# Gate maps of a PEER block: five of eight scaled one-hot rows on VectorE, none on GpSimd, all evictions on ScalarE

## The reference

```python
def peer(h, w_pq, sub_keys, expert_u, expert_v):
    q = (h @ w_pq).reshape(B, S, PEER_HEADS, 2, PEER_QHALF)          # 8 heads
    s = jnp.einsum('bshjd,hjnd->bshjn', q, sub_keys)
    v1, i1 = lax.top_k(s[..., 0, :], 16)
    v2, i2 = lax.top_k(s[..., 1, :], 16)
    ...                                                             # 16 best sums v1 + v2
    idx = ...                                                       # i1 * 128 + i2 of the chosen
    gate = jax.nn.softmax(top_s, axis=-1)
    ...
    a = jnp.einsum('tkd,td->tk', expert_u[idx], h)
    w = gate * jax.nn.gelu(a)
    return jnp.einsum('tk,tkd->td', w, expert_v[idx])
```

## Time and profile before

| | us |
|---|---|
| median of 3 runs | 2202.58 (2202.4 to 2205.08) |
| the profiled execution, its own time | 2205.34 |
| its span, first to last instruction | 2203.6 |
| gates stage, first one-hot work to last eviction | 729.66 to 897.94, that is 168.28 |
| engines busy over the span | PE 91%, DVE 60%, ACT 31%, POOL 23% |

### The profile page before, as it was taken

One profiled execution on the slowest core, in us unless ns is written; L12 is line 12 of the kernel. 1 busy time (PEld: TensorE's weight loads), 2 busy tenths in 40 slices (PEclk: granted clock), 3 DMA queues, 4 the chain that ended last, 5 costly groups with the idle time before them and its releaser, 6 DMA issues.

```text
span 2203.6 us, 25778 instructions
## 1 busy us (share of the span) xinstructions
PE 2012.5 (91%) x9280; PEld 1654.8 (75%) x9280; DVE 1316.8 (60%) x2260; ACT 679.1 (31%) x1074; POOL 499.6 (23%) x305
## 2 busy tenths in 40 slices
PE   5998876969987777899999999999999999999997
PEld 4777555747775777788788888888888888888886
DVE  6545677349997899655445544554555455445544
ACT  4113342342322788412222212222221222122212
POOL 1877424027776677100000000000000000000000
PEclk7899678979998999999999999999999999999999
DMA  8243000422232666754322422342233224322430
GB/s 320 105 191 153 1 0 3 150 95 71 78 115 86 210 206 196 251 187 151 131 95 95 172 113 95 114 171 95 95 137 149 95 95 152 133 95 95 168 118 38
DMA packets 124158, 276.65 MB, mean 126 GB/s; under 512 B 4816, under 2 KB 70352, under 8 KB 116560
## 3 DMA queue, kind: packets, MB, share of 16 engines
q1 hardware_dynamic: 124112, 276.10, 34.5%
HBM read 233.10 MB, written 42.99 MB: 125 GB/s over the span
## 4 chain that ended last, share of the span: by engine, by line
PE 58%; DVE 0%; ACT 0%; DVEq 0%; issue 0%; ACTq 0%
PE bank L1815 27%; PE bank L1841 26%; PE bank L1830 6%; DVE u_raw L1802 0%; DVE rows L1788 0%; ACT L1727 0%; DVE u L1736 0%; DVEq L1588 0%; ACT u L1680 0%; ACT v_raw L1723 0%; DVE rows L1768 0%; DVE rows L1779 0%; ACT act_out L1705 0%; ACTq L1588 0%; DVE rstd L1798 0%
## 5 line engine op out<-in xcount | busy, mean ns | idle before, releaser
L1815 PE MATMUL bank<-actT,u 128*128 128x512 f32 x2592 | 593.7, 390 | 6.9 <-DVE u L1736 4.2
L1841 PE MATMUL bank<-v_parts,w 128*128 128x512 f32 x2496 | 570.0, 389 | 0.0
L1815 PEld LDWEIGHTS bank<-actT,u 128*128 128x128 f32 x2592 | 487.6, 188 | 108.7 <-DVE u L1736 4.3
L1841 PEld LDWEIGHTS bank<-v_parts,w 128*128 128x128 f32 x2496 | 468.6, 188 | 97.1
L1768 DVE TENSOR_TENSOR rows<-rows,bank 128x512 f32<-128x512 f32 x208 | 142.4, 687 | 256.8 <-PE bank L1841 256.8
L1687 ACT ACTIVATE v_parts<-v_raw 128x1024 fp32r<-128x1024 f32 x104 | 109.7, 1055 | 450.9 <-DVE rows L1768 450.4
L1388 PE MATMUL bank<-actT,hl 128*128 128x512 f32 x864 | 212.8, 406 | 31.0 <-POOL hl L1238 27.7
L1747 DVE TENSOR_TENSOR weighed<-act_out,group_gates 128x512 f32<-128x512 f32 x105 | 72.7, 692 | 270.9 <-ACT act_out L1691 270.9
L1388 PEld LDWEIGHTS bank<-actT,hl 128*128 128x128 f32 x864 | 167.6, 197 | 70.1 <-POOL hl L1238 18.2
L1744 DVE TENSOR_TENSOR v_parts<-v_raw,v_parts 128x1024 fp32r<-128x1024 f32 x128 | 156.3, 1221 | 91.9 <-DMA group_gates<-expert_gates 32.3
L1691 ACT ACTIVATE act_out<-bank 128x512 f32<-128x512 f32 x104 | 62.2, 598 | 401.9 <-PE bank L1815 401.9
(11 more groups left out here) (239 smaller groups left out, 2039.3 us busy)
## 6 DMA issues: line engine op xcount, KB each, us to landing
u_raw<-in_u SPq DMA_DIRECT2D x27, 2048.0 KB, 7.4
v_raw<-in_v SPq DMA_DIRECT2D x26, 2048.0 KB, 7.4
expert_gates<-gates SPq DMA_DIRECT2D x16, 2048.0 KB, 8.7
group_gates<-expert_gates SPq DMA_DIRECT2D x32, 1024.0 KB, 6.8
wada<-in_w_ada SPq DMA_DIRECT2D x24, 1024.0 KB, 6.7
v_raw<-in_v SPq DMA_DIRECT2D x24, 512.0 KB, 3.5
raw<-in_u SPq DMA_DIRECT2D x20, 512.0 KB, 3.5
raw<-in_w_cols SPq DMA_DIRECT2D x16, 512.0 KB, 7.3
```

The source lines that it names most:

```text
L1815: last = nc.tensor.matmul(m.psum[j % banks][:], u[:, p, j, kc * P:(kc + 1) * P], m.actT[:, q, kc, :], start=(kc == 0 and i == 0), stop=(kc ...
L1841: last = nc.tensor.matmul(m.psum[2 + p % 6][:], w[:, x, j, t * P:(t + 1) * P], v[:, z, j, half * S:(half + 1) * S], start=(j == 0 and i == 0),
```

## The change

GpSimd has no work in the stage any more. Of the 8 scaled rows of a round, VectorE makes tokens 0 to 4 directly, with one instruction each that compares `iota` with the slot's first key and multiplies by the slot's gate (both as one value per partition); ScalarE scales tokens 5 to 7. `first_hits` shrinks from 8 tokens to those 3. ScalarE evicts both halves of the result, and VectorE none. The core of the diff:

```diff
-        m.iota_bf = sb("iota_bf", [P, NKEY, ROUND], BF16)
+        m.iota_bf = sb("iota_bf", [P, NKEY, ACT_ROWS], BF16)
...
-ACT_ROWS = 4
+VEC_ROWS = 5
+ACT_ROWS = ROUND - VEC_ROWS
...
-        hits = sb("first_hits", [P, BUFS, NKEY, ROUND], BF16)
+        hits = sb("first_hits", [P, BUFS, NKEY, ACT_ROWS], BF16)
...
-        @block.gpsimd
-        def _(pool):
...
-                    nc.gpsimd.tensor_tensor(
-                        onehot1[:, b % BUFS, 0:pool_n, :].rearrange("p t k -> p k t"), hits[:, b % BUFS, :, 0:pool_n],
-                        slotsT[:, 2, n].unsqueeze(1).to_broadcast([P, NKEY, pool_n]), ALU.mult
-                        ).then_inc(pool_rows, 1)
...
-                for u in range(pool_n, ROUND):
+                for u in range(VEC_ROWS, ROUND):
                     at = (i * rounds + b) * ROUND + u
-                    last = nc.scalar.activation(onehot1[:, b % BUFS, u, :], hits[:, b % BUFS, :, u], ACT.Copy,
+                    last = nc.scalar.activation(onehot1[:, b % BUFS, u, :], hits[:, b % BUFS, :, u - VEC_ROWS], ACT.Copy,
                                                 scale=slotsT[:, 2, at:at + 1])
...
+                for c in range(CHUNKS):
+                    act.wait_ge(gated, i * (rounds * CHUNKS) + (b * CHUNKS + c + 1))
+                    at = b * ROUND % TB + c * PER
+                    nc.scalar.activation(gates[:, k, :, at:at + PER],
+                                         m.psum[CHUNKS * (b % BUFS) + c][:].rearrange("p (t j) -> p j t", t=PER),
+                                         ACT.Copy).then_inc(gates_read, 1)
...
+                late = slice(r * ROUND + VEC_ROWS, (r + 1) * ROUND)
                 V.tensor_tensor(hits[:, b % BUFS], iota_bf[:],
-                                first_bf[:, n].unsqueeze(1).to_broadcast([P, NKEY, ROUND]), ALU.is_equal
+                                first_bf[:, late].unsqueeze(1).to_broadcast([P, NKEY, ACT_ROWS]), ALU.is_equal
                                 ).then_inc(hits_ready, 1)
+                for u in range(VEC_ROWS):
+                    at = r * ROUND + u
+                    last = V.tensor_scalar(onehot1[:, b % BUFS, u, :], iota[:], slotsT[:, 0, at:at + 1],
+                                           slotsT[:, 2, at:at + 1], ALU.is_equal, ALU.mult)
+                last.then_inc(vec_rows, 1)
...
-                if r >= 2:
-                    read_second_half(r - 2)
...
-                    pe.wait_ge(pool_rows, i * rounds + (b + 1))
+                    pe.wait_ge(vec_rows, i * rounds + (b + 1))
...
-                        if c == pool_n // PER:
+                        if c == VEC_ROWS // PER:
                             pe.wait_ge(act_rows, i * rounds + (b + 1))
```

More of the change, by code:

```diff
@@ L1215, in _ @@
             g = nc.gpsimd
-            for out, pattern in ((places, [[1, NCAND]]), (m.iota, [[1, NKEY]]), (m.iota_bf, [[1, NKEY], [0, ROUND]])):
+            for out, pattern in ((places, [[1, NCAND]]), (m.iota, [[1, NKEY]]), (m.iota_bf, [[1, NKEY], [0, ACT_ROWS]])):
                 g.iota(out[:], pattern, base=0, channel_multiplier=0,
@@ L1456, in stage_gates @@
         hits_ready, second_ready = sem("hits_ready"), sem("second_ready")
-        pool_rows, act_rows = sem("pool_rows"), sem("act_rows")
+        vec_rows, act_rows = sem("vec_rows"), sem("act_rows")
         gated = sem("gated")
-        gates_read = [sem("gates_read_by_act"), sem("gates_read_by_dve")]
+        gates_read = sem("gates_read")
         stored = m.stored
@@ L1462, in stage_gates @@
         rounds = 2 * TB // ROUND
-        pool_n = ROUND - ACT_ROWS
         block = own.enter_context(nc.Block())
-        @block.gpsimd
-        def _(pool):
[L1468 to L1474, removed]
-                    nc.gpsimd.tensor_tensor(
-                        onehot1[:, b % BUFS, 0:pool_n, :].rearrange("p t k -> p k t"), hits[:, b % BUFS, :, 0:pool_n],
-                        slotsT[:, 2, n].unsqueeze(1).to_broadcast([P, NKEY, pool_n]), ALU.mult
-                        ).then_inc(pool_rows, 1)
-            body(0, True)
-            with pool.Fori(1, pairs) as i:
-                body(i, False)
         @block.scalar
@@ L1523, in _ @@
                 for k in range(2):
-                    for c in range(CHUNKS):
-                        sp.wait_ge(gates_read[c], p * (2 * TB // ROUND) + ((k + 1) * (TB // ROUND)))
+                    sp.wait_ge(gates_read, p * (2 * TB // PER) + ((k + 1) * (TB // PER)))
                     dst = a.gates[:, 0:NKEY * S].rearrange("p (g n) -> p g n", n=NTB * JG * TB)
@@ L1532, in _ @@
             m.dve.then(dve, V.tensor_copy(first_bf[:], slotsT[:, 0, :]))
[L1534 to L1543, removed]
             for r in range(pairs * rounds):
@@ L1554, in _ @@
                                 ).then_inc(second_ready, 1)
-                if r >= 2:
-                    read_second_half(r - 2)
-            for r in range(pairs * rounds - 2, pairs * rounds):
-                read_second_half(r)
         @block.tensor
@@ L1567, in body @@
                         if not (first and b < BUFS):
-                            pe.wait_ge(gates_read[c], i * rounds + (b - BUFS + 1))
-                        if c == pool_n // PER:
+                            pe.wait_ge(gates_read, i * (rounds * CHUNKS) + ((b - BUFS) * CHUNKS + c + 1))
+                        if c == VEC_ROWS // PER:
                             pe.wait_ge(act_rows, i * rounds + (b + 1))
```

## The result

The changed kernel took 2220.32 us (median of 7 runs, 2216.34 to 2225.1), the one before 2205.95 in the same 7 rounds. The ratio is 1.0065, 95% interval 1.0046 to 1.0083: slower by 14.3 us (10.1 to 18.3). The profiled execution took 2216.34, 11.0 above the profiled one of before.

A forecast was written before the change was run, and what follows sets the result against it. VectorE was taken to bound the gates stage: 0.28 + 1.26 + 1.13 = 2.67 us a round against 2.578, over 63 rounds +5.8, last round -0.35, so +5.45: 2208.0 against the median 2202.58. Range 2204 to 2222.

The forecast's parts named there:

- The main case's own range: Whole program: 2205 to 2212 us around 2208.0, from 0.01 on each small instruction and on the period; chance 0.57.
- the slower hits: Rival on VectorE's hits in the gates stage: slowed in part or fully, program at 2211 to 2223 us; chance 0.22.
- VectorE's round is the period after: Gates stage: VectorE's instructions, 2.67 us a round against 2.578, set the period, with no gap on VectorE.
- The five rows, 0.252 each, 1.26: VectorE's five new compare-and-multiply instructions a round: 0.252 us each from start to start, 1.26 together.
- the rival in which the second value costs nothing: VectorE's new rows at the one-value price of 0.197 us each, ScalarE's 2.44 the period, program 2193.4; chance 0.09.
- The hits, 0.28: VectorE's hits, 384 elements for 1024, at two elements a cycle: 0.28 us a round from start to start.
- the slow case: VectorE's hits at one element a cycle: 0.48 us for 0.28, 12.8 us more, program 2220.8; within a 0.22 chance.
- The last round, -0.35: End of the gates stage: from the last hits to the last eviction 5.50 us for 5.85, so -0.35.
- The other engines hide the eviction: Gates stage: the second eviction moves to ScalarE, 2.44 us a round under VectorE's 2.67, so it costs nothing.
- The stage's shift goes through one for one: Behind the gates stage: a shift of its end moves the program's end equally, the map's load hidden by some 9 us.
- VectorE's instructions of a round, end to end, are the period; the other engines follow: Gates stage of the kernel before: hits 0.85, `onehot2` 1.13 and copy 0.60 on VectorE make 2.578 us a round.
- The copy that I valued at 0.60: VectorE's copy of a result half in each round of the gates stage: its removal was to save 0.60 us.

The follow-up runs named there:

- v4: Changed kernel with VectorE making 4 scaled rows for 5 and ScalarE 4 for 3; ratio 0.9979 against the kernel before.
- onevalue: Changed kernel with the gate left out of VectorE's five rows, the second value being the constant 1.0; 2200.72 us against the changed kernel's 2222.2.
- evenstart: Changed kernel with ScalarE taking tokens 0 to 2 and VectorE 3 to 7, so the hits' run starts on an even element; 2220.11 us in one run.
- a0: The changed kernel itself, run again as yardstick; ratio 1.0064 against the kernel before.
- ghost: Changed kernel with GpSimd multiplying in each round into a tile that nobody reads; 2264.79 us in one run.
- pool5: Kernel before with ScalarE evicting both halves, GpSimd making 5 rows for 4 and ScalarE 3 for 4; ratio 1.0143 against the kernel before.
- v4_again: Changed kernel with 4 rows on VectorE and 4 on ScalarE, run a second time; ratio 0.9985 against the kernel before.
- evict: Kernel before with ScalarE evicting both halves and VectorE none, all else as before; ratio 1.0004 against the kernel before.
- mix: Changed kernel with rows split VectorE 3, GpSimd 2, ScalarE 3, and `onehot2` right after the hits; ratio 1.0111 against the kernel before.

## Why the prediction was right, and where it was not

The direction and the range held: 2220.32 in 2204 to 2222, slower. The size was too small: +5.45 us forecast, +14.3 (10.1 to 18.3) measured. The main case's own range, 2205 to 2212, was missed. The wide range held in part by luck: it was that wide for the slower hits, and these account for 3.8 us (63 x 0.06); 2.7 of the rest come from an effect behind the stage that no rival named. By its steps:

1. *VectorE's round is the period after.* Right: no idle time ahead of any of its lines, 2.75 a round, and v4 and onevalue move the program by what they take off VectorE's sum.
2. *The five rows, 0.252 each, 1.26.* 1.28, 0.256 each. L547's four-times longer form gave the price within 2%; the rival in which the second value costs nothing is refuted by onevalue (0.06 each, with 0.196 for one value where the old row had 0.197).
3. *The hits, 0.28.* 0.34. Mis-sized, and three tenths of the way to the slow case: neither full speed nor one element a cycle (0.48). The run of 3 is what costs; the odd start, which I named beside it, does not (evenstart). The rule of a 4-byte aligned start in the Trainium skill ("Advanced Engine Details and Errata", 2x-1p Requirements), by which this would have been the slow form, isn't what is seen: 0.34 with either start. Nor is my main case, in which a pair of elements may span two odd runs at no cost.
4. *The last round, -0.35.* +0.16 here, -0.10 in a0 (5.75). TensorE starts 0.24 after `onehot2`'s recorded end, where I had 0.05 from GpSimd's. The other 0.26 are in the record alone: in this execution VectorE's durations had grown by then, and its starts are 2.749 apart for 2.7535 in a0, with the same 179.22 for the stage.
5. *The other engines hide the eviction.* Right, with more room than I gave: ScalarE's scalings fell to 0.392 of duration from 0.520, at steps of 6 bytes for 16. GpSimd's absence isn't the reason: with GpSimd at work they take 0.392 at 6 bytes (ghost) and 0.523 at 16 (pool5).
6. *The stage's shift goes through one for one.* Nearly: 2.7 us more come behind it, a clock effect whose cause is open. In the two profiled executions the stage also began 2.7 us earlier in the one of after, which hides it there in the span; such differences of the earlier stages come and go between executions of one kernel (728.0 for the first hits in a0, 735.5 in v4, 730.1 in v4_again).

Steps 3 and 2 make 63 x 0.08 = 5.0, step 4 0.5; with 5.45 that is the stage's 10.9. The 2.7 of step 6 brings it to 13.6 of the 14.3, the rest lies in the interval.

One step was right in its number and wrong in its reason: "VectorE's instructions of a round, end to end, are the period; the other engines follow", of the kernel before. 0.24 of its 0.85 for the hits was time in which they were held. The real loop was hits (the part after GpSimd, 0.49), 0.25 to GpSimd's start, GpSimd's 1.84: 2.58. That 1.84 seems to be stretched in turn by `onehot2`, which it lies beside: an instruction of as many elements, with an fp32 source, takes 1.11 in ghost, where it doesn't; no run isolates this. A row of the kernel before shows the hold too, and I overlooked it. In the stage's second round VectorE has no copy yet, and the hits and `onehot2` alone fill 734.00 - 731.41 = 2.59:

```profile
731.41 1.53 DVE L1549 TENSOR_TENSOR first_hits<-iota_bf,first_bf 128x1024 bf16<-128x1024 bf16 x1
732.86 1.21 DVE L1552 TENSOR_TENSOR onehot<-iota,slotsT 128x1024 f32<-128x1024 f32 x1
734.00 1.52 DVE L1549 TENSOR_TENSOR first_hits<-iota_bf,first_bf 128x1024 bf16<-128x1024 bf16 x1
```

The copy that I valued at 0.60 shortened no round of VectorE by going as long as GpSimd did its 4 rows (evict), and 0.24 of the hits couldn't be had with GpSimd there. Only both together gave what the sum takes off (1.17 in it, 1.11 as measured), so the sum came out near because the change did both. That was luck.

The change loses because 1.28 and 0.34 replace 0.85 and 0.60: 0.17 more on the engine that bounds the stage, while ScalarE is left with some 0.5 a round unused. One row fewer on VectorE turns the loss into a gain of 0.15 to 0.2%.

## What to carry to other kernels

An engine that shows as busy without a gap may be held inside its instructions. Compare the duration of one form in different places (here 0.69 with GpSimd idle, 0.93 and 1.53 beside it), and look whether its end keeps a fixed distance from another engine's end; if it does, removing other work from the engine may give nothing. When work is shared out anew among engines, add up the instructions from start to start, then move the split by one unit either way: 5 + 3 lost 0.65%, 4 + 4 gained 0.15 to 0.2%.

## What the runs showed of the hardware

- VectorE's bf16 compare and its small compare-and-multiply hardly advance beside a two-input GpSimd instruction: the hits ended 0.49, 0.51 and 0.54 us after GpSimd's instructions of 1.84, 1.82 and 2.27, where they take 0.61 from start to start alone. The Trainium skill ("Advanced Engine Details and Errata", VectorE Performance Modes) says that the second port of VectorE is shared with GpSimd and that GpSimd and "2p" instructions block each other; the five rows agree (+0.87 beside 1.17), if they run in the 2p mode that its table allows them. The hits have two sources, which run in no 2p mode by that page, and are held as well; another section of the page (GPSIMD Details) counts instructions with two inputs in SBUF among those in conflict, and they agree with that. `onehot2` has two as well. It starts 0.33 ahead of GpSimd's instruction and keeps its 1.21 (evict, mix), and there GpSimd's is the one that gets longer, 1.58 for 0.97.
- A compare of 384 bf16 elements in runs of 3 takes as long as one of 512 in runs of 4, 0.34 from start to start, and one of 640 in runs of 5 takes 0.47. Whether the run starts on an odd or an even element makes no difference.
- A second value per partition costs a compare-and-multiply of 128 fp32 elements 0.06 us: 0.256 for 0.196.
- The end of a recorded duration is firmer than its start: in the profiled execution after the change VectorE's durations grew by 0.25 over the stage (hits 0.42 to 0.67) while the starts crept ahead by 63 x 0.0041 = 0.26 against a0, where the durations stayed at 0.41; the stage took 179.22 in both.
